# Three paired steps in each gated network instead of two, with the input's sums and two of four weight sums on GpSimd

## The chip, the core and the metric

The kernel runs on one core of a Trainium2 chip. The metric is the device time of one execution in microseconds (us), the median of several runs; lower is better. The engines are TensorE (PE in the profile, PEld for its weight loads), VectorE (DVE), ScalarE (ACT), GpSimd (POOL) and SyncE (SP, which issues the loads here). Each has its own instruction stream, worked off in order; they meet only at semaphores. PSUM is the memory that TensorE writes to (`bank` in the names); the rest of the tiles lie in SBUF.

## The reference

The program computes a block with four mixers and a mixture of experts, and then two layers of a second block. Each layer of the second block runs a gated network, a mixer and a second gated network. Those four gated networks, called ffn0 to ffn3, are what the change touches:

```python
def swiglu(x, w_gate, w_up, w_down):
    return (jax.nn.silu(x @ w_gate) * (x @ w_up)) @ w_down
# second block, both layers: 256 tokens, D_MODEL = 1024, D_FF = 2816, float32
f = swiglu(rms_norm_2(x, g[0]), ffn_w_gate[layer, 0], ffn_w_up[layer, 0], ffn_w_down[layer, 0])
x = x + 0.5 * rms_norm_2(f, g[1])
... # mixer_ab in layer 0, mixer_c in layer 1
f = swiglu(rms_norm_2(x, g[4]), ffn_w_gate[layer, 1], ffn_w_up[layer, 1], ffn_w_down[layer, 1])
x = x + 0.5 * rms_norm_2(f, g[5])
```

## The kernel before

**Split products.** Weights and activations are float32. Each operand is split into a high part (a rounded copy, made by ScalarE, `split` at L994) and a low part (the rest, a subtraction on VectorE, L1718), and a product is the sum of three matmuls: high by high, high by low, low by high. A low part costs VectorE one `tensor_tensor` of 128x2048 with both inputs in SBUF.

**Units.** All weights come as units of 1 MB (128 x 2048 float32). SyncE loads them in their order into a ring of 5 slots (`ring`), each once its slot is released: by default when the low part of the unit that lay there has been made (`RELEASE`, `load`). A network has 11 steps (`FFN_STEPS`) of 256 hidden columns. Step s uses two gate-and-up units (`place_A`: 3s-1 and 3s) and one down unit (`place_D`: 3s+4).

**A plain step** (`gate_up`, `turn`, `down_tile`). Per token tile t (0 or 1) TensorE does 24 matmuls of 128x512 for gate and up; ScalarE takes the silu, VectorE multiplies (`hid_made`, L2336); TensorE transposes the hidden values (`turn`, L3440), ScalarE and VectorE split them (`hid_in`, `hid_left`); 24 matmuls multiply by the down unit of the step before. Together 72 matmuls.

**A paired step** (`pair`, at the steps in `PAIRS`, 3 and 7 before) takes two steps, s and s+1, as a 2x2 block product: 2 token tiles by 2 column blocks, over 2 halves of the inner dimension. It uses seven block products where two plain steps use eight (Strassen's scheme in Winograd's form). A block product (`product`, L3483 to L3485) is 12 matmuls. For this it needs sums of the input blocks (`x_whole`, `x_sums`, `x_left`, once per network) and, per pair, four sums of the weight blocks b11, b21, b12, b22, which are the units a, a+1, a+3, a+4: t1 = b12 - b11 into the tile `w_sum` (which is `F`); t3 = b22 - b12 in b12's slot; t2 = t3 + b11 in b11's slot; t4 = b21 - t2 in b21's slot. t1 and t3 are made by `weight_sums` (L2371, L2373), t2 and t4 by `more_weight_sums` (L2378, L2380), all on VectorE in the step ahead of the pair. ScalarE makes the high parts of the sums in the single tile `sum_hi` in the order t2, t4, t1; VectorE the low parts (`ring_left`, `sum_left`, L2385).

The order of a pair on TensorE is: product with b11 (bank 4); `turn`; m6 (with t2; waits for its low part); product with b21; m7 (with t3; waits for `u2`, the sum that empties bank 7 into c_12); down, tile 0; m4 (with t4; waits for `u3`, the sum into c_22); down, tile 1; product with b22 (bank 4); `turn`; m5 (with t1; waits for its low part); down of step s. Semaphores `ffn_dve`, `ffn_act` and `ffn_pe` count each engine's steps by the lists `FFN_DVE`, `FFN_ACT`, `FFN_PE`. In the order of the program, "the step ahead" is the plain step right before a pair; with pairs at 3 and 7, two plain steps (5 and 6) lie between them.

GpSimd does only small things in this stretch: the root of the norms on 128x1 tiles (`post_power`, L876 to L882).

Of the kernel before, what the change touches and what calls it, by code (L numbers as in the profile page):

```python
# [5 lines left out]
FP32 = mybir.dt.float32  # L6
# [46 lines left out]
PAIRS = (3, 7)  # L53
# [217 lines left out]
def build(nc, x, gains, stream, small_1, cmp_w1, small_2, consts, slots, out):  # L271
# [3 lines left out]
    with ExitStack() as ctx:  # L275
# [524 lines left out]
        def _(sp):  # L800
# [66 lines left out]
        def _(pool):  # L867
# [89 lines left out]
        def _(act):  # L957
# [353 lines left out]
            def sparse():  # L1311
# [34 lines left out]
                for s in range(SPARSE_STEPS):  # L1346
# [4 lines left out]
                    act.activation(sil_m[:, :], bank[4][:, 0:UC], ACT.Silu, scale=rc[:, 6 * i + 4:6 * i + 5]).then_inc(S("m_silu"), 1)  # L1351
# [20 lines left out]
            def gated(name):  # L1372
# [20 lines left out]
                def x_sums_high():  # L1393
                    act.wait_ge(S("ffn_dve"), ffn_at(FFN_DVE, name, "s4"))
# [8 lines left out]
                def pair(i, s):  # L1403
# [10 lines left out]
                    split_at(3 * s + 4)  # L1414
                    act.wait_ge(S("ffn_pe"), ffn_at(FFN_PE, name, f"m4_{i}"))
# [22 lines left out]
                for s in range(1, last):  # L1438
# [7 lines left out]
                    silu(s, 1)  # L1446
                    if s + 1 in PAIRS:
# [3 lines left out]
                    if s + 2 == PAIRS[0]:  # L1451
                        x_sums_high()
# [252 lines left out]
        def _(dve):  # L1705
# [493 lines left out]
            def sparse():  # L2199
# [125 lines left out]
            def gated(name):  # L2325
# [23 lines left out]
                def x_whole():  # L2349
                    dve.wait_ge(S("h_lo"), HI0[name] + 4)  # L2350
# [1693 lines left out]
```

## Time and profile before

| | |
|---|---|
| median of 3 runs | 1794.06 us (1793.16 to 1794.82) |
| the profiled execution | 1793.34 us, span 1790.4 us |
| TensorE busy | 98% of the span |
| VectorE busy | 78% |
| ScalarE busy | 56% |
| GpSimd busy | 3% |
| the networks in the span | about 717 to 886, 1088 to 1256, 1273 to 1441, 1611 to 1780 us |

The time beside the span is 2.94 us. Busy time says that an engine had an instruction in hand. A matmul's duration (0.39 us) overlaps that of the next; what a matmul costs is the distance between two starts. The four networks run alike, to the same waits, so the working below follows one of them, ffn1, on its own clock.

### The profile page before, as it was taken

What the parts mean: (1) busy time and instruction counts of PE and PEld (TensorE: products, weight loads), DVE (VectorE), ACT (ScalarE), POOL (GpSimd) and SP (SyncE); (2) the same over time, 40 slices, a digit from 0 to 9 for tenths busy, and PEclk for the clock granted to TensorE, in tenths of its full rate; (3) what the DMA queues carried; (4) which work ended last, traced back from release to release, by engine and by line L of the source; (5) the groups of instructions that cost most, each with busy time, mean ns of one, the idle gap of its engine ahead of it and who ended that gap; (6) DMA issues with size and microseconds to landing.
All of it is one profiled execution on the core that took longest, in us unless ns stands there. A gap on an engine that the chain in (4) does not pass through costs nothing.

```text
span 1790.4 us, 25225 instructions
## 1 busy us (share of the span) xinstructions
PE 1754.3 (98%) x10314; PEld 1482.6 (83%) x10314; DVE 1389.7 (78%) x1646; ACT 995.0 (56%) x1206; POOL 58.1 (3%) x98
## 2 busy tenths in 40 slices
PE   9999999999999999999999999999999999999998
PEld 8998898888888887787898988778877878787877
DVE  5349877788898898978498779886897667879784
ACT  5446653577777676645452355555555456656453
POOL 0040000000000001000000000000100010010000
PEclk9999999999999999999999999999999999999999
DMA  9343344699899897373442016527443745234631
GB/s 383 118 165 136 119 148 149 240 359 351 337 351 354 334 372 293 123 280 139 190 152 108 27 53 230 225 83 312 180 170 136 305 143 187 72 141 150 273 147 76
DMA packets 51379, 363.01 MB, mean 203 GB/s; under 512 B 5697, under 2 KB 5825, under 8 KB 8642
## 3 DMA queue, kind: packets, MB, share of 16 engines
q1 hardware_dynamic: 50976, 359.24, 52.6%
q8 instruction: 82, 1.34, 0.3%
q10 hardware_dynamic: 290, 2.17, 0.3%
q14 instruction: 31, 0.25, 0.0%
HBM read 360.34 MB, written 1.05 MB: 202 GB/s over the span
## 4 chain that ended last, share of the span: by engine, by line
PE 79%; DVE 15%; ACT 3%; issue 1%; DMA 1%; POOL 0%; DVEq 0%; POOLq 0%; ACTq 0%
PE bank L2866 8%; PE bank L3424 4%; PE bank L3426 4%; PE bank L3425 4%; PE bank L3451 3%; PE bank L3449 3%; PE bank L3450 3%; PE bank L3278 3%; PE bank L3280 3%; PE bank L3279 3%; DVE w_a L1718 3%; PE bank L3483 3%; PE bank L2924 3%; PE bank L3484 2%; PE bank L3485 2%; PE bank L3295 2%
## 5 line engine op out<-in xcount | busy, mean ns | idle before, releaser
L1718 DVE TENSOR_TENSOR w_a<-ring,w_a 128x2048 fp32r<-128x2048 f32 x220 | 500.4, 2287 | 132.5 <-ACT w_a L994 131.8
L994 ACT ACTIVATE w_a<-ring 128x2048 fp32r<-128x2048 f32 x219 | 416.2, 1913 | 121.4 <-PE bank L3451 42.1
L1718 DVE TENSOR_TENSOR w_b<-ring,w_b 128x2048 fp32r<-128x2048 f32 x63 | 144.1, 2287 | 29.3 <-ACT w_b L994 29.2
L994 ACT ACTIVATE w_b<-ring 128x2048 fp32r<-128x2048 f32 x63 | 120.5, 1912 | 36.2 <-PE bank L3426 17.8
L2866 PE MATMUL bank<-h,w_a 128*128 128x256 f32 x1040 | 137.3, 285 | 1.0 <-DVE ring_lo L1823 1.0
L2866 PEld LDWEIGHTS bank<-h,w_a 128*128 128x128 f32 x1040 | 128.8, 191 | 4.1 <-issue 3.0
L3449 PE MATMUL bank<-w_a,hid 128*128 128x512 f32 x280 | 109.9, 393 | 0.0
L3451 PE MATMUL bank<-w_a,hid 128*128 128x512 f32 x280 | 109.2, 390 | 0.0
L3450 PE MATMUL bank<-w_a,hid 128*128 128x512 f32 x280 | 109.0, 389 | 0.0
L3424 PE MATMUL bank<-w_a,h 128*128 128x512 f32 x240 | 95.0, 396 | 0.5 <-DVE w_a L1718 0.5
L3426 PE MATMUL bank<-w_a,h 128*128 128x512 f32 x240 | 93.7, 390 | 0.0
L3425 PE MATMUL bank<-w_a,h 128*128 128x512 f32 x240 | 93.4, 389 | 0.0
L1391 ACT ACTIVATE sil<-bank,tiny 128x256 f32<-128x256 f32 x64 | 30.4, 474 | 101.0 <-PE bank L3426 98.9
L3278 PE MATMUL bank<-w_a,xg 128*128 128x512 f32 x192 | 77.1, 402 | 0.0
L3280 PE MATMUL bank<-w_a,xg 128*128 128x512 f32 x192 | 75.0, 391 | 0.0
L3279 PE MATMUL bank<-w_a,xg 128*128 128x512 f32 x192 | 74.8, 390 | 0.0
L978 ACT ACTIVATE arena<-bank 128x512 f32<-128x512 f32 (+2 forms) x47 | 26.8, 571 | 74.8 <-PE bank L2866 54.8
L881 POOL TENSOR_SCALAR tiny<-tiny 128x1 f32<-128x1 f32 x20 | 10.7, 533 | 1588.7 <-ACT junk L1012 1002.4
L3451 PEld LDWEIGHTS bank<-w_a,hid 128*128 128x128 f32 x280 | 52.6, 188 | 11.2
L2336 DVE SCALAR_TENSOR_TENSOR hid<-bank,tiny,sil 128x256 f32<-128x256 f32 x64 | 30.7, 480 | 39.9 <-ACT sil L1391 39.9
L3450 PEld LDWEIGHTS bank<-w_a,hid 128*128 128x128 f32 x280 | 52.6, 188 | 10.9
L3449 PEld LDWEIGHTS bank<-w_a,hid 128*128 128x128 f32 x280 | 52.6, 188 | 10.8
(648 smaller groups left out, 4201.1 us busy)
## 6 DMA issues: line engine op xcount, KB each, us to landing
ring<-in_stream SPq DMA_DIRECT2D x330, 1024.0 KB, 5.3
G<-in_gains SPq DMA_DIRECT2D x14, 512.0 KB, 7.8
cmp_area<-in_cmp_w ACTq DMA_DIRECT2D x1, 2048.0 KB, 11.3
sm<-in_small SPq DMA_DIRECT2D x1, 1582.0 KB, 12.0
con<-in_consts SPq DMA_DIRECT2D x1, 1032.0 KB, 15.9
X<-in_x SPq DMA_DIRECT2D x2, 512.0 KB, 4.0
out_x<-X SPq DMA_DIRECT2D x4, 256.0 KB, 2.0
sm<-in_small SPq DMA_DIRECT2D x1, 730.5 KB, 22.5
```

The costliest lines, as they stand in the source:

```text
L994: act.activation(w_slot(unit)[:, 0, :], ring[:, unit % RING, :], ACT.Copy).then_inc(S("w_hi"), 1)
L1718: dve.tensor_tensor(w_slot(unit)[:, 1, :], ring[:, unit % RING, :], w_slot(unit)[:, 0, :].bitcast(FP32), ALU.subtract).then_inc(S("w_lo"), 1)
L2866: ins = pe.matmul(ps, w(wp, k), xp[:, k, :], start=(a == 0 and k == 0), stop=(a == 2 and k == terms - 1))
L3278: pe.matmul(bank[4][:, :], x_hi, w[0][:, k, :], start=(half == 0 and k == 0), stop=False)
L3279: pe.matmul(bank[4][:, :], x_hi, w[1][:, k, :], start=False, stop=False)
L3280: ins = pe.matmul(bank[4][:, :], x_lo, w[0][:, k, :], start=False, stop=(half == 1 and k == 3))
L3424: pe.matmul(bank[4 + t][:, :], x_hi, w[0][:, k, :], start=first, stop=False)
L3425: pe.matmul(bank[4 + t][:, :], x_hi, w[1][:, k, :], start=False, stop=False)
L3426: ins = pe.matmul(bank[4 + t][:, :], x_lo, w[0][:, k, :], start=False, stop=end)
L3449: pe.matmul(ps, x_hi, w[0][:, f, d], start=(s == 0 and f == 0), stop=False)
L3450: pe.matmul(ps, x_hi, w[1][:, f, d], start=False, stop=False)
L3451: return pe.matmul(ps, x_lo, w[0][:, f, d], start=False, stop=(s == last and f == 1))
```

## The change

The pairs move from the steps 3 and 7 to the steps 2, 5 and 8, so only one plain step lies between two pairs, one (step 1) ahead of the first, and step 10 is the last. The five instructions that form the input's sums, and t3 and t1 of each pair, move from VectorE to GpSimd (`pair_sums`, called after `post_power` of the network). t1 is now formed as b22 - t2, which is the same sum; it waits for m6, and the slots of b11 and b22 are released to SyncE only once it is done. t2's low part goes to `w_sum_lo` (the tile `y_2`) instead of the ring. ScalarE makes the input sums' high part behind the second silu of step 1, and VectorE the low part there, ahead of t2, where both stood at the end of that step before. The semaphore `ffn_pool` counts GpSimd's steps; in the experts it stands in for `m_silu`.

```diff
-PAIRS = (3, 7)
+PAIRS = (2, 5, 8)
...
-                RELEASE[b11] = ("ffn_pe", ffn_at(FFN_PE, name, f"m6_{i}"))
+                SUMMED[b22] = ffn_at(FFN_POOL, name, f"t1_{i}")
+                RELEASE[b11] = ("ffn_pool", ffn_at(FFN_POOL, name, f"t1_{i}"))
                 RELEASE[b21] = ("ffn_pe", ffn_at(FFN_PE, name, f"m4_{i}"))
...
+            def pair_sums(name):
+                pool.wait_ge(S("h_lo"), HI0[name] + 4)
+                pool.tensor_tensor(x_raw, h_hi[:, :, :].bitcast(FP32), h_lo[:, :, :].bitcast(FP32), ALU.add).then_inc(S("ffn_pool"), 1)
+                own(name, "x_raw")
...
+                pool.tensor_tensor(x_sum[:, 0], a21, a22, ALU.add).then_inc(S("ffn_pool"), 1)
...
+                for i, s in enumerate(PAIRS):
+                    b11, _, b12, b22 = pair_units(name, s)
+                    for b in (b12, b22):
+                        pool.wait_ge(S(f"unit{b % RING}"), 16 * (b // RING + 1))
+                    pool.tensor_tensor(ring[:, b12 % RING, :], ring[:, b22 % RING, :], ring[:, b12 % RING, :], ALU.subtract)\
+                        .then_inc(S("ffn_pool"), 1)
+                    pool.wait_ge(S("ffn_dve"), ffn_at(FFN_DVE, name, f"t2_{i}"))
+                    pool.wait_ge(S("ffn_pe"), ffn_at(FFN_PE, name, f"m6_{i}"))
+                    pool.tensor_tensor(w_sum, ring[:, b22 % RING, :], ring[:, b11 % RING, :], ALU.subtract).then_inc(S("ffn_pool"), 1)
...
@@ scalar, gated
                     silu(s, 1)
+                    if s + 1 == PAIRS[0]:
+                        x_sums_high()
                     if s + 1 in PAIRS:
                         pair_ahead(PAIRS.index(s + 1), s + 1)
...
@@ vector, gated
-                    if s + 2 == PAIRS[0]:
-                        x_whole()
-                    if ahead is not None:
-                        weight_sums(ahead, s + 1)
                     split_at(3 * s + 3)
                     hid_made(s, 1)
+                    if s + 1 == PAIRS[0]:
+                        x_left()
                     if ahead is not None:
                         more_weight_sums(ahead, s + 1)
-                        ring_left(f"t2_hi_{ahead}", pair_units(name, s + 1)[0])
+                        sum_left(f"t2_hi_{ahead}", w_sum_lo, ring[:, pair_units(name, s + 1)[0] % RING, :])
...
@@ tensor, pair
-                    product(7, both[1], (sum_hi[:, :], ring_lo[:, b11 % RING, :]), True).then_inc(S("ffn_pe"), 1)
+                    product(7, both[1], (sum_hi[:, :], w_sum_lo), True).then_inc(S("ffn_pe"), 1)
```

GpSimd's instructions in ffn1, after the root of the norm (`tiny`), in the program after; before, nothing stands between that root and the next network's. `sm` holds the whole input, `H` its sums, `ring` the units, `F` is t1.

```order
L882 TENSOR_TENSOR tiny<-tiny 128x1 [waits s_pool_chain]
L952 TENSOR_TENSOR sm<-h 128x2048 [waits s_h_lo]
L955 TENSOR_TENSOR H<-sm 128x512 [waits s_ffn_pool]
L957 TENSOR_TENSOR H<-H,sm 128x512 [waits s_ffn_pool]
L958 TENSOR_TENSOR H<-sm 128x512
L960 TENSOR_TENSOR H<-sm,H 128x512 [waits s_ffn_pool]
L965 TENSOR_TENSOR ring<-ring 128x2048 [waits s_unit0,s_unit4]
L969 TENSOR_TENSOR F<-ring 128x2048 [waits s_ffn_pe,s_ffn_dve]
L965 TENSOR_TENSOR ring<-ring 128x2048 [waits s_unit4,s_unit3]
```

Seven instructions of 128x2048 and four of 128x512 per network are new on this engine, and t1 of a pair stands ahead of t3 of the next.

VectorE in ffn1 of the program before, from the second product of hidden values of step 0 (`hid<-bank5`) to the first input sums at the end of step 1; L1718 is a split.

```order
L2336 SCALAR_TENSOR_TENSOR hid<-bank5,tiny,sil 128x256 [waits s_silu]
L1718 TENSOR_TENSOR w_a<-ring,w_a 128x2048 [waits s_w_hi]
L2336 SCALAR_TENSOR_TENSOR hid<-bank4,tiny,sil 128x256 [waits s_silu]
L2343 TENSOR_TENSOR hid_2<-bank6,hid_2 128x2x256 [waits s_hid_hi]
L2351 TENSOR_TENSOR sm1<-h_2 128x2048 [waits s_h_lo]
L1718 TENSOR_TENSOR w_a<-ring,w_a 128x2048 [waits s_w_hi]
L2336 SCALAR_TENSOR_TENSOR hid<-bank5,tiny,sil 128x256 [waits s_silu]
L1718 TENSOR_TENSOR w_b<-ring,w_b 128x2048 [waits s_w_hi]
L2357 TENSOR_TENSOR H<-sm1 128x512 [waits s_ffn_dve]
```

The same place after (L1752 is now the split, L2370 and L2377 the hidden values): behind the second hidden values of step 1 stand the low part of the input sums (L2401), t2 and t4 (L2387, L2389), and t2's low part (L2394), because the first pair now follows this step.

```order
L2370 SCALAR_TENSOR_TENSOR hid<-bank5,tiny,sil 128x256 [waits s_silu]
L1752 TENSOR_TENSOR w_a<-ring,w_a 128x2048 [waits s_w_hi]
L2370 SCALAR_TENSOR_TENSOR hid<-bank4,tiny,sil 128x256 [waits s_silu]
L2377 TENSOR_TENSOR hid_2<-bank6,hid_2 128x2x256 [waits s_hid_hi]
L1752 TENSOR_TENSOR w_a<-ring,w_a 128x2048 [waits s_w_hi]
L2370 SCALAR_TENSOR_TENSOR hid<-bank5,tiny,sil 128x256 [waits s_silu]
L2401 TENSOR_TENSOR f_hi<-H,xs_hi 128x2048 [waits s_ffn_act]
L2387 TENSOR_TENSOR ring<-ring 128x2048 [waits s_unit1,s_ffn_pool]
L2389 TENSOR_TENSOR ring<-ring 128x2048 [waits s_ffn_dve]
L2394 TENSOR_TENSOR y_2<-ring,sum_hi 128x2048 [waits s_ffn_act]
L1752 TENSOR_TENSOR w_b<-ring,w_b 128x2048 [waits s_w_hi]
```

What moved: the sum of the whole input has left, the input sums' low part now waits for GpSimd through ScalarE right before the pair, and t2 waits for GpSimd's t3.

## Rows read from the trace of the kernel before

**Rows 1.** The page: busy us (share) xinstructions; the granted TensorE clock by slices.
```profile
PE 1754.3 (98%) x10314; PEld 1482.6 (83%) x10314; DVE 1389.7 (78%) x1646; ACT 995.0 (56%) x1206; POOL 58.1 (3%) x98
PEclk9999999999999999999999999999999999999999
```
**Rows 2.** Windows, ffn1: stretch, us, then busy us (x) per engine, clock, DMA.
```profile
1078.00:1256.00 178.00, 175.59 (x794) 144.03 (x793) 140.98 (x108) 94.94 (x84) 2.94 (x4) 1.00 0.55 213
```
**Rows 3.** Waits of TensorE: total us, times, longest us.
```profile
PE bank L3483 <- DVE ring_lo L2385: 9.6, 8, 1.4
```
**Rows 4.** Timeline of TensorE, ffn1: start us, duration us, instruction, idle before.
```profile
1088.03 0.39 PE L3424 MATMUL bank<-w_a,h 128*128 128x512 f32 x1
...
1093.25 0.39 PE L3426 MATMUL bank<-w_b,h 128*128 128x512 f32 x1
...
1104.82 0.39 PE L3424 MATMUL bank<-w_a,h 128*128 128x512 f32 x1
...
1124.35 0.60 PE L3440 MATMUL bank<-con,hid 128*128 128x128 f32 x4
1126.30 0.50 PE L3483 MATMUL bank<-sum_hi,xs_hi 128*128 128x512 f32 x1 [1.36 <-DVE ring_lo L2385]
```
**Rows 5.** Timeline of VectorE, first pair of ffn1.
```profile
1119.44 2.28 DVE L2378 TENSOR_TENSOR ring<-ring 128x2048 f32<-128x2048 f32 x1
1121.75 2.29 DVE L2380 TENSOR_TENSOR ring<-ring 128x2048 f32<-128x2048 f32 x1
...
1128.37 2.28 DVE L1718 TENSOR_TENSOR w_b<-ring,w_b 128x2048 fp32r<-128x2048 f32 x1
1130.57 0.68 DVE L2343 TENSOR_TENSOR hid<-bank,hid 128x512 fp32r<-128x512 f32 x1
...
1131.77 2.28 DVE L1718 TENSOR_TENSOR w_a<-ring,w_a 128x2048 fp32r<-128x2048 f32 x1
1133.97 0.48 DVE L2336 SCALAR_TENSOR_TENSOR hid<-bank,tiny,sil 128x256 f32<-128x256 f32 x1
1134.36 2.28 DVE L2385 TENSOR_TENSOR ring_lo<-ring,sum_hi 128x2048 fp32r<-128x2048 f32 x1
1136.56 0.68 DVE L2395 TENSOR_TENSOR sm<-bank,sm 128x512 f32<-128x512 f32 x1
```
**Rows 6.** Timeline of ScalarE, same pair.
```profile
1134.27 1.92 ACT L994 ACTIVATE w_a<-ring 128x2048 fp32r<-128x2048 f32 x1 [1.67 <-DMA ring<-in_stream]
1140.52 1.92 ACT L1416 ACTIVATE sum_hi<-F 128x2048 fp32r<-128x2048 f32 x1 [4.33 <-PE bank L3485]
```
**Rows 7.** Timeline of GpSimd, around 110 us, where it works beside VectorE.
```profile
107.07 2.00 POOL L925 TENSOR_TENSOR arena<-arena 128x1084 f32<-128x1084 f32 x1
109.14 1.54 POOL L930 TENSOR_TENSOR arena<-arena 128x810 f32<-128x810 f32 x1
...
119.19 0.94 POOL L930 TENSOR_TENSOR arena<-arena 128x264 f32<-128x264 f32 x1
120.21 1.08 POOL L933 TENSOR_TENSOR arena<-arena,con 128x16 f32<-128x16 f32 x1
...
123.43 0.73 POOL L937 TENSOR_TENSOR arena<-arena 128x256 f32<-128x256 f32 x1
```
**Rows 8.** Timeline of VectorE, the same stretch.
```profile
109.68 1.28 DVE L1840 TENSOR_SCALAR arena<-arena,tiny 128x512 f32<-128x512 f32 x1
...
119.44 1.78 DVE L1823 TENSOR_TENSOR ring_lo<-ring,w_a 128x1024 fp32r<-128x1024 f32 x1
...
121.14 1.23 DVE L1823 TENSOR_TENSOR ring_lo<-ring,w_a 128x1024 fp32r<-128x1024 f32 x1
```
**Rows 9.** Timeline of VectorE and GpSimd, start of ffn1.
```profile
1084.01 2.28 DVE L1718 TENSOR_TENSOR w_a<-ring,w_a 128x2048 fp32r<-128x2048 f32 x1
1084.49 1.87 POOL L876 TENSOR_SCALAR tiny<-tiny 128x1 f32<-128x1 f32 x1 [6.07 <-ACT junk L1147]
1086.44 0.56 POOL L877 TENSOR_TENSOR tiny<-tiny 128x1 f32<-128x1 f32 x1
1088.03 2.29 DVE L1718 TENSOR_TENSOR w_b<-ring,w_b 128x2048 fp32r<-128x2048 f32 x1 [1.32 <-ACT w_b L994]
```

More of the change, by code:

```diff
@@ L738, in sums_ready @@
             return "unit_used", D_UNITS[of] + (3 * STEPS[of] if of in STEPS else SQUARE)
+        SUMMED = {}
         for name in FFNS:
             for i, s in enumerate(PAIRS):
-                b11, b21, _, _ = pair_units(name, s)
-                RELEASE[b11] = ("ffn_pe", ffn_at(FFN_PE, name, f"m6_{i}"))
+                b11, b21, _, b22 = pair_units(name, s)
+                SUMMED[b22] = ffn_at(FFN_POOL, name, f"t1_{i}")
+                RELEASE[b11] = ("ffn_pool", ffn_at(FFN_POOL, name, f"t1_{i}"))
                 RELEASE[b21] = ("ffn_pe", ffn_at(FFN_PE, name, f"m4_{i}"))
@@ L939, in _, with own @@
                 src, dst = dst, src
+            def own(name, step):
+                pool.wait_ge(S("ffn_pool"), ffn_at(FFN_POOL, name, step))
+            def pair_sums(name):
+                pool.wait_ge(S("h_lo"), HI0[name] + 4)
+                pool.tensor_tensor(x_raw, h_hi[:, :, :].bitcast(FP32), h_lo[:, :, :].bitcast(FP32), ALU.add).then_inc(S("ffn_pool"), 1)
+                own(name, "x_raw")
+                a11, a12, a21, a22 = (x_raw[:, 4 * j:4 * j + 4, t * P:(t + 1) * P] for t in range(TT) for j in range(2))
+                pool.tensor_tensor(x_sum[:, 0], a21, a22, ALU.add).then_inc(S("ffn_pool"), 1)
+                own(name, "s1")
+                pool.tensor_tensor(x_sum[:, 1], x_sum[:, 0], a11, ALU.subtract).then_inc(S("ffn_pool"), 1)
+                pool.tensor_tensor(x_sum[:, 2], a11, a21, ALU.subtract).then_inc(S("ffn_pool"), 1)
+                own(name, "s2")
+                pool.tensor_tensor(x_sum[:, 3], a12, x_sum[:, 1], ALU.subtract).then_inc(S("ffn_pool"), 1)
+                for i, s in enumerate(PAIRS):
[7 more added lines that the diff above has]
+                    pool.tensor_tensor(w_sum, ring[:, b22 % RING, :], ring[:, b11 % RING, :], ALU.subtract).then_inc(S("ffn_pool"), 1)
             post_power("moe")
-            for name in ("ffn0", "ab"):
-                post_power(name)
+            post_power("ffn0")
+            pair_sums("ffn0")
+            post_power("ab")
             pool.wait_ge(S("x_turned"), 4 * NB["ab"] + 4)
@@ L948, in _ @@
             pool.memset(glu[:, :, 0:CONV_B - 1], 0.0).then_inc(S("zeroed_2"), 1)
-            for name in ("ffn1", "ffn2", "c"):
+            for name in ("ffn1", "ffn2"):
                 post_power(name)
-            for name in ("ffn3", "end"):
-                post_power(name)
+                pair_sums(name)
+            post_power("c")
+            post_power("ffn3")
+            pair_sums("ffn3")
+            post_power("end")
         @block.scalar
```

46 lines of the change are left out of this document (11 added, 35 removed).

## The prediction

> **What bounds the kernel now.** I read the busy shares first, then the granted clock, then TensorE's waits, then the timelines of one network. TensorE is busy for 98% of the span, and no slice shows a lowered clock [rows 1]. In ffn1 it is busy for 175.6 of 178.0 us, VectorE for 141.0 [rows 2]. So the networks run at TensorE's pace: 24 matmuls start from 1088.03 to 1093.25, 5.22 us over 23 distances, so a matmul costs 0.227 us [rows 4]. The only wait of note inside a pair is m6 for t2's low part: 9.6 us in eight pairs, 2.4 us per network [rows 3]. The reader should see that VectorE is not far behind, and that within a pair its chain is tight: a sum ends at 1123.96+2.28, and m6 starts at 1126.30 [rows 4, 5].
>
> All sums below are made against the profiled execution, 1793.34 us (0.7 us under the median of the runs). I count as no change what lies within 0.2%, or 3.6 us.
>
> **What the change saves.** A third pair per network replaces eight block products by seven: 12 matmuls of 0.227 us, 2.7 us per network. The old waits at m6 (2.4 us per network) are removed from the sum here and counted again below as they will then be. VectorE loses the sum of the whole input, four of 128x512 and two of 128x2048 per pair (2.28 us each, as those in [rows 5]), but that is worth only what TensorE waits for.
>
> **What GpSimd's instructions cost.** On GpSimd 128x1084 took 2.00 us and 128x256 took 0.73 us with little beside them [rows 7]. A line through both gives 1.53 ns per element, 3.5 us for 2048; in proportion to the 2.07 us between the starts of the first two it would be 3.9. I take 3.6 us for 128x2048 and 1.1 us for 128x512 (0.73 + 256 x 1.53 ns).
>
> **Do the two engines run side by side?** This decides the case. Four places say no, where VectorE reads two SBUF operands. At 119.44 a split of 128x1024 took 1.78 us, its twin at 121.14 took 1.23: it was held for 0.55 us, while GpSimd's instruction from 119.19 ran to 120.13 [rows 7, 8]. The `tensor_scalar` at 109.68 took 1.28 us and ended at 110.96, just after GpSimd's of 109.14 had ended at 110.68 [rows 7, 8]. The other way round, a 128x16 of GpSimd at 120.21 took 1.08 us, till that split had ended [rows 7, 8], and a 128x1 at 1084.49 took 1.87 us, till VectorE's split of 1084.01 ended at 1086.29 [rows 9]. So whoever started first keeps the other out for the whole instruction, and they take turns. VectorE instructions with an operand in PSUM (`hid_made`, `hid_left`, the sums into c) I take as not held.
>
> The Trainium skill says the same (SBUF — State Buffer, "SBUF: two separate sides"): the port pair is an exclusive lock, for a VectorE instruction with two SBUF inputs too, when the GpSimd one reads SBUF. That speaks against this change, since a sum moved away from VectorE blocks it for longer than it took there. It also gives 4497 ns for a GpSimd `tensor_tensor` of 2048 elements (GPSIMD Engine Reference, 3.1 Elementwise); no row here has that size. By it every hold below is 0.9 us longer, about 6 us more per network, and the sum would be some 25 us higher.
>
> **The start of a network**, ffn1's clock. GpSimd is free at 1087.0 [rows 9] and takes the whole input, 1087.1 to 1090.7. The split of unit 3, at 1088.03 before [rows 9], is held: 1090.7 to 1092.95. TensorE wants it after 12 matmuls from 1088.03, at 1090.75: a wait of 2.2 us. Then they take turns: input sum 1 to 1094.1, split to 1096.3, hidden values of tile 1 to 1096.8. TensorE's `turn`, due at 1093.5 + 2.2 = 1095.7, waits 1.1 us more. Together 3.3 us.
>
> **The first m6.** The turns go on: sum 2 to 1097.5, split 5 to 1099.7, sum 3 to 1100.9, sum 4 to 1102.1, split 6 to 1104.35, t3 on GpSimd to 1107.95. Now VectorE's low part of the input sums (to 1110.2), t2 (1112.4), t4 (1114.6) and t2's low part, to 1116.85, each 2.2 us from start to start. TensorE starts the pair at 1104.82 [rows 4] + 3.3 = 1108.1, does a product (2.7) and the transposes (0.35) and is ready for m6 at 1111.2. It waits 5.7 us. Without any hold the chain would still be late: high part of the input sums after the silu at 1100.1 to 1102.0, then 2.2 x 4 = 8.8 to 1110.8, against 1107.9: 2.9 us. From above, 0.9 us more per GpSimd instruction of 2048 gives 8.
>
> **The second and third m6.** VectorE no longer makes t1 and t3 ahead of the split of b21, so t2 could start 1.2 us sooner than at 1119.44. But only one plain step now lies ahead, and b22's load waits for a slot that is released late in the last pair; it lands in the middle of the step, so t3 (3.6 us) holds the split of b21 by about 1.0 us. I get a wait of 1.2 us each, as now; bounds 0.2 (no hold) and 3. 2.4 us per network.
>
> **m4 in each pair.** Count from the start of m6. VectorE makes two splits (to 4.4), GpSimd's t1 has been ready since 2.9 (m6 done) and runs 4.4 to 8.0; `hid_left` and u2 pass beside it (to 5.6); the split of b22 is held from 5.6 to 8.0 and ends at 10.2; hidden values (10.6), t4's low part (12.8), u3 (13.5). Before, the same chain ran without the hold, from 1131.77 to 1137.24 [rows 5]. TensorE is at m4 after m6, b21, m7 and down, four times 2.72, at 10.9. It waits 2.6 us, three times: 7.8 us per network. Lower bound 0 (no hold), upper 3.5 each. The unit in b11's slot is loaded only when t1 is done, 5 us later than before in the pair. ScalarE waited for it already, 1.67 us to 1134.27, but had then to wait for m4 until 1140.52 [rows 6], 4.3 us of cover, and m4 itself is late: I count nothing. If this cover goes, m5 is up to 3 us late.
>
> **The end.** The gain rows share memory with `sum_hi`, so SyncE's loads of gains and of the last two units wait for the last m5, now a pair later, in step 9 instead of 8. ScalarE and VectorE then split them behind; by my count they are just in time for the last down products. I take 0; up to 2 us per network if not.
>
> **Sum.** Per network 3.3 + 5.7 + 2.4 + 7.8 = 19.2 us of waits, less 2.4 of old waits, less 2.7 of matmuls: +14.1 us. Times four, +56: 1793.3 + 56.4 = 1849.7 us. I say 1850.
>
> **Rivals.**
> - *The engines run side by side after all*, at least for these instructions, the point from which it decides being any hold under about 0.5 us. Then per network the first m6 waits 2.9, the others 0.2, m4 0: 3.3 - 2.4 - 2.7 = -1.8, four times -7: 1786 us. For it: no row has two instructions of 2048 elements against each other. Against: [rows 7 to 9]. This is the faster side, 7%.
> - *The holds are there but VectorE's slack takes most of them.* It is idle for 37 of 178 us in ffn1 [rows 2], and a wait of TensorE at one place gives it time for the next. If m4's wait is 1 us and the start and first m6 cost 5 together: 5 + 2.4 + 3 - 5.1 = 5.3, times four: 1815 us. Against: VectorE's chain inside a pair has no gap of note before m4. 14%.
> - *The clock falls.* A wait of 5.7 us is four times the longest now at m6 [rows 3], and no slice shows a lowered clock now [rows 1]. If TensorE fell from 2.4 to 1.2 GHz behind each first m6 and lost, say, one block product's time (2.7 us) in going at half speed, 4 x 2.7 = 11 us: 1861. With longer holds beside it, up to 1880. 16%. The Trainium skill (TensorE: Matmul & The Clock Gate, Part 1) says that idleness lowers the clock; no row here shows it.
> - *The change doesn't show*: gains and holds cancel within 3.6 us. 3%.
>
> **How the numbers follow.** The forecast of holds as summed has 60%, with its own range 1838 to 1875 (a hold 0.4 us shorter or 0.9 longer in each of seven places per network, four times). For 8 in 10 I take in most of the clock's case and the upper part of the slack's: 1812 to 1880. Slower: 0.60 + 0.14 + 0.16 = 0.90, same 0.03, faster 0.07.
>
> **What would show it.** GpSimd's sums with starts and ends against VectorE's splits: splits of 128x2048 lasting up to 5.9 us instead of 2.28, GpSimd's 128x2048 at 3.5 us or more. TensorE's waits: m6 about 5.7 us in the first pair and 1 to 2 in the others; a new one at m4 of about 2.6 us, twelve times; one of 2 us in step 1. If splits stay at 2.28 us beside GpSimd, the forecast's main step is wrong. If TensorE's waits total under 10 us more than before, the sizes are.

## The result, and the profile after

The changed kernel takes 1892.45 us (median of 4 runs, 1890.68 to 1898.52), the kernel before 1793.61 us beside it (4 runs). The ratio is 1.056, 95% interval 1.054 to 1.058: about 99 us slower. The forecast was 1850 us with 1812 to 1880. The direction was right, and the time lies 12 us above the range. The profiled execution took 1893.17 us, its span is 1891.4 us.

The page, against [rows 1]:

```profile
PE 1779.3 (94%) x10266; PEld 1494.1 (79%) x10266; DVE 1497.8 (79%) x1654; ACT 1019.3 (54%) x1222; POOL 232.1 (12%) x142
PEclk9999999999999998999999999999899999999999
```

48 matmuls fewer, and yet TensorE is busy 25.0 us longer; it is idle 112.1 us (1891.4 - 1779.3) instead of 36.1. So of 101.0 us more span, 76.0 are new waits. The other 25.0 are slower work, with the 10.8 us (four times 2.7) that 48 matmuls fewer save already taken off. By the prediction it would have been 67.2 us of waits (4 x 19.2 less 9.6) and 10.8 less of work. VectorE is busy 108.1 us longer, although the input's sums, t3 and t1 were taken from it: in this view the duration of an instruction includes the time for which it is held.

TensorE's waits (total us, times, longest), against [rows 3]; L3486 is the product of both m6 (`y`, the low part of t2) and m4 (`sm`, u3), L3427 the gate products, L3443 the `turn`:

```profile
PE bank L3486 <- DVE y L2394: 49.5, 12, 6.3
PE bank L3486 <- DVE sm L2404: 22.4, 12, 2.0
PE bank L3427 <- DVE w_a L1752: 6.8, 2, 3.9
...
PE bank L3427 <- DVE w_b L1752: 2.9, 1, 2.9
PE bank L3443 <- DVE hid L2370: 2.3, 1, 2.3
```

All the waits that the prediction named are there, in its places; only at the start there is one wait per network, of 2.3 to 3.9 us, where it had two (2.2 and 1.1). Now the groups of instructions (busy us, mean ns of one | idle before):

```profile
L1752 DVE TENSOR_TENSOR w_a<-ring,w_a 128x2048 fp32r<-128x2048 f32 x220 | 574.5, 2624 | 143.9 <-ACT w_a L1027 143.2
...
L969 POOL TENSOR_TENSOR F<-ring 128x2048 f32<-128x2048 f32 x12 | 56.7, 4723 | 181.4 <-PE bank L3488 181.4
L965 POOL TENSOR_TENSOR ring<-ring 128x2048 f32<-128x2048 f32 x12 | 55.4, 4618 | 255.2 <-DMA ring<-in_stream 255.2
...
L955 POOL TENSOR_TENSOR H<-sm 128x512 f32<-128x512 f32 x4 | 12.8, 3209 | 0.3
```

The mean split rose from 2287 to 2624 ns. GpSimd needs 4.6 to 4.7 us for 128x2048, where the prediction took 3.6. The first two of its 128x512 last 3.2 us each, but the last one takes 1.30 us, with no split beside it (the row at 1126.31 below): the rest is waiting for a split. Both engines in ffn1, first VectorE, then GpSimd (start us, duration us, instruction, idle before), against [rows 5] and [rows 9]:

```profile
1112.90 5.72 DVE L1752 TENSOR_TENSOR w_b<-ring,w_b 128x2048 fp32r<-128x2048 f32 x1 [1.32 <-ACT w_b L1027]
1118.54 3.36 DVE L1752 TENSOR_TENSOR w_a<-ring,w_a 128x2048 fp32r<-128x2048 f32 x1
...
1128.51 5.82 DVE L1752 TENSOR_TENSOR w_a<-ring,w_a 128x2048 fp32r<-128x2048 f32 x1 [2.33 <-ACT w_a L1027]
...
1149.92 6.31 DVE L1752 TENSOR_TENSOR w_a<-ring,w_a 128x2048 fp32r<-128x2048 f32 x1
...
1187.45 5.62 DVE L1752 TENSOR_TENSOR w_b<-ring,w_b 128x2048 fp32r<-128x2048 f32 x1 [3.43 <-ACT w_b L1027]
```

```profile
1111.85 4.62 POOL L952 TENSOR_TENSOR sm<-h 128x2048 f32<-128x2048 f32 x1
1116.55 3.21 POOL L955 TENSOR_TENSOR H<-sm 128x512 f32<-128x512 f32 x1
...
1126.31 1.30 POOL L960 TENSOR_TENSOR H<-sm,H 128x512 f32<-128x512 f32 x1
1127.56 4.62 POOL L965 TENSOR_TENSOR ring<-ring 128x2048 f32<-128x2048 f32 x1
...
1149.35 4.73 POOL L969 TENSOR_TENSOR F<-ring 128x2048 f32<-128x2048 f32 x1 [17.16 <-PE bank L3488]
...
1186.31 4.61 POOL L965 TENSOR_TENSOR ring<-ring 128x2048 f32<-128x2048 f32 x1 [32.23 <-DMA ring<-in_stream]
```

Read them in pairs. GpSimd's sum of 1127.56 ends at 1132.18; the split of 1128.51 lasts till 1134.33, 2.15 us more, which is about its own 2.28. The distance of the two ends is 2.15 us for 1111.85 with 1112.90, for 1149.35 with 1149.92 and for 1186.31 with 1187.45, too. A VectorE instruction with an operand in PSUM isn't held: one of 128x512 (u2) started at 1205.11, inside GpSimd's sum from 1205.00 to 1209.72, and took its usual 0.68 us. None of those that run inside a GpSimd sum in this trace takes over 0.7 us.

The waits at the end of that, on TensorE, against [rows 4], and four stretches (length, then busy us and count of PE, PEld, DVE, ACT, POOL, then the granted clock, DMA share, GB/s), against [rows 2]:

```profile
1143.71 0.80 PE L3486 MATMUL bank<-sum_hi,xs_hi 128*128 128x512 f32 x1 [5.92 <-DVE y L2394]
...
1200.25 0.50 PE L3486 MATMUL bank<-sum_hi,xs_hi 128*128 128x512 f32 x1 [3.52 <-DVE y L2394]
```

```profile
1119.00:1122.00 3.00, 3.00 (x8) 2.32 (x8) 3.00 (x2) 0.00 (x0) 2.92 (x2) 0.50 0.73 251
1144.00:1148.00 4.00, 4.00 (x10) 3.13 (x10) 4.00 (x3) 3.44 (x4) 0.00 (x0) 0.50 0.00 0
1148.00:1152.00 4.00, 4.00 (x15) 3.16 (x15) 3.35 (x4) 1.92 (x1) 2.65 (x1) 0.81 0.00 0
1152.00:1156.00 4.00, 4.00 (x19) 3.23 (x18) 4.00 (x1) 0.47 (x1) 2.08 (x1) 1.00 0.26 37
```

Behind the wait of 2.9 us in step 1 and behind the 5.9 us at m6, TensorE runs at 0.50 of its clock, 1.2 GHz: 10 matmuls start in 4 us where 19 do at full clock. The page's digit per slice (47 us) hides that. In the 4 us behind each of the twelve waits at m6, those of 2.5 us too, the mean clock is 0.50 to 0.69; behind those at m4, of 1.6 to 2.0 us, it stays at 1.00. Added up from 700 us on, (1 - clock) x busy time is 34 us; before, it is 3.4 us over the whole span.

### The profile page after: what moved, and what is told of

It is laid out like the page before. It is cut to its first block, busy times and chain, and to the rows that moved or that the text cites. A ratio compares the mean times of both kernels' runs of the same rounds, so it can differ in the third digit from the quotient of the medians.

```text
span 1891.4 us, 25277 instructions
## 1 busy us (share of the span) xinstructions
PE 1779.3 (94%) x10266; PEld 1494.1 (79%) x10266; DVE 1497.8 (79%) x1654; ACT 1019.3 (54%) x1222; POOL 232.1 (12%) x142
## 3 DMA queue, kind: packets, MB, share of 16 engines
HBM read 360.34 MB, written 1.05 MB: 191 GB/s over the span
## 4 chain that ended last, share of the span: by engine, by line
PE 66%; DVE 23%; ACT 4%; issue 4%; DMA 2%; POOL 1%; DVEq 0%; POOLq 0%; ACTq 0%
PE bank L2869 7%; DVE w_a L1752 7%; PE bank L3281 3%; PE bank L3283 3%; PE bank L3282 3%; DVE w_b L1752 3%; PE bank L2927 2%; PE bank L3486 2%; PE bank L3427 2%; PE bank L3454 2%; PE bank L3429 2%; PE bank L3428 2%; PE bank L3452 2%; PE bank L3453 2%; PE bank L3487 2%
## 5 line engine op out<-in xcount | busy, mean ns | idle before, releaser
L1752 DVE TENSOR_TENSOR w_a<-ring,w_a 128x2048 fp32r<-128x2048 f32 x220 | 574.5, 2624 | 143.9 <-ACT w_a L1027 143.2
L1752 DVE TENSOR_TENSOR w_b<-ring,w_b 128x2048 fp32r<-128x2048 f32 x63 | 174.4, 2768 | 32.6 <-ACT w_b L1027 32.4
L886 POOL TENSOR_SCALAR tiny<-tiny 128x1 f32<-128x1 f32 x20 | 10.7, 535 | 1078.4 <-ACT junk L1045 491.9
L3486 PE MATMUL bank<-sum_hi,xs_hi 128*128 128x512 f32 x96 | 49.8, 519 | 49.5 <-DVE y L2394 49.5
L965 POOL TENSOR_TENSOR ring<-ring 128x2048 f32<-128x2048 f32 x12 | 55.4, 4618 | 255.2 <-DMA ring<-in_stream 255.2
L3427 PE MATMUL bank<-w_a,h 128*128 128x512 f32 x192 | 77.4, 403 | 6.8 <-DVE w_a L1752 6.8
L969 POOL TENSOR_TENSOR F<-ring 128x2048 f32<-128x2048 f32 x12 | 56.7, 4723 | 181.4 <-PE bank L3488 181.4
L3429 PE MATMUL bank<-w_a,h 128*128 128x512 f32 x192 | 76.0, 396 | 0.0
L3428 PE MATMUL bank<-w_a,h 128*128 128x512 f32 x192 | 75.9, 395 | 0.0
L1434 ACT ACTIVATE sum_hi<-ring 128x2048 fp32r<-128x2048 f32 x12 | 23.0, 1914 | 85.4 <-DVE ring L2387 85.4
L3486 PEld LDWEIGHTS bank<-sum_hi,xs_hi 128*128 128x128 f32 x96 | 23.2, 242 | 57.1 <-DVE y L2394 52.3
## 6 DMA issues: line engine op xcount, KB each, us to landing
sm<-in_small SPq DMA_DIRECT2D x1, 730.5 KB, 22.4
```

Of the source, the lines that this page charges most:

```text
L1752: dve.tensor_tensor(w_slot(unit)[:, 1, :], ring[:, unit % RING, :], w_slot(unit)[:, 0, :].bitcast(FP32), ALU.subtract).then_inc(S("w_lo"), 1)
L3427: pe.matmul(bank[4 + t][:, :], x_hi, w[0][:, k, :], start=first, stop=False)
L3428: pe.matmul(bank[4 + t][:, :], x_hi, w[1][:, k, :], start=False, stop=False)
L3429: ins = pe.matmul(bank[4 + t][:, :], x_lo, w[0][:, k, :], start=False, stop=end)
```

## The experiments

The theory: a GpSimd instruction that reads SBUF and a VectorE instruction with two SBUF inputs take turns; this makes VectorE's chain late at three places (the start, m6, m4), and the clock adds to it. The rivals were that GpSimd's results merely come late, that three pairs are too dense in themselves, and that the clock, not VectorE, makes the pair long. The kernel before ran beside each, with medians of 1791.4 to 1794.1 us, and the ratios are to these.

**Is it the turns, and what do three pairs cost without them?**

`small_sums`: GpSimd's sums cover 16 columns.

```diff
-pool.tensor_tensor(w_sum, ring[:, b22 % RING, :], ring[:, b11 % RING, :], ALU.subtract)
+pool.tensor_tensor(w_sum[:, 0:16], ring[:, b22 % RING, 0:16], ring[:, b11 % RING, 0:16], ALU.subtract)
...
-act.activation(xs_hi[:, :, :, :], x_sum, ACT.Copy)
+act.activation(xs_hi[:, :, :, :], other(h_hi), ACT.Copy)
```

> The changed kernel with each of GpSimd's sums cut to its first 16 columns; every wait and every place stays, so the products run on values that are not the sums (the high and low parts of the input sums and of t1 are taken from other tiles of the same size). Theory H (a GpSimd sum shuts VectorE's two-input instructions out for its whole length, and the waits that this makes let TensorE's clock fall): the holds are gone, splits last 2.28 us, m4 waits about 0, the first m6 about 3 us, the others under 0.5, the clock falls little: 1780 to 1792 us. Theory S (the layout does it: one plain step between pairs, a slot released late, input sums' parts right ahead of the first pair, whatever engine makes the sums): waits of 4 us at m6 and 2 us at m4 stay, 1870 us or more.

1791.49 us (10 runs), ratio 0.9998 (0.9987 to 1.0009). Span 1787.6 us, and the waits:

```profile
PE bank L3490 <- DVE y L2398: 13.0, 12, 2.8
```

The first m6 of each network waits 2.83 us, as worked out for the chain without a hold (2.9), the others 0.19 to 0.29; m4 waits for nothing and starts 11.22 us after m6. So the third pair is worth next to nothing even with sums that cost nothing, and all of the loss comes from what GpSimd's sums do.

`writes_only`, `writes_longer` and `writes_same`: the sums are replaced by GpSimd writing a constant to the same tiles, with the same waits, for about 3.7, 5.6 and 4.8 us per 128x2048. A write reads nothing.

```diff
-pool.tensor_tensor(w_sum, ring[:, b22 % RING, :], ring[:, b11 % RING, :], ALU.subtract)
+for n in range(FILLS):   # 2; 3; 2 and one of 1100 columns
+    pool.memset(w_sum, 0.0)
```

> The changed kernel with each of GpSimd's sums replaced by two fills (memset) of the same tile, one after the other: GpSimd is busy for about 3.8 us for 128x2048 instead of 4.6, and reads nothing of SBUF; the sums are zero, so the products are. Theory H in the form that only a GpSimd instruction that reads SBUF shuts VectorE out: splits stay at 2.28 us beside it, m4 waits about 0, only t3 and the input sums come late: 1785 to 1800 us. Theory H in the form that any GpSimd instruction on SBUF shuts it out: splits of up to 5 us, m4 waits about 1.5 us, 1850 us or more. Theory S: 1870 or more, whatever the form.

1791.67 us (10 runs), ratio 1.0 (0.999 to 1.0011); splits at 2287 ns.

> As the run with two fills per sum, but with three, 5.4 us for 128x2048, longer than the 4.6 us of the real sum. If only reading shuts VectorE out: splits at 2.28 us, TensorE waits a little longer at the first m6 for t3; 1790 to 1805 us. If it was the shorter time of the two fills that made that run fast: 1830 us or more.

1830.3 us (1827.88 to 1836.71), ratio 1.0224 (1.0203 to 1.0244). That is above the expected range of 1790 to 1805 us: splits still take 2288 ns, but the waits are back.

```profile
PE bank L3492 <- DVE y L2400: 27.0, 12, 3.9
PE bank L3449 <- DVE hid L2376: 16.5, 12, 1.5
```

The lateness of GpSimd's results alone can thus cost, if it is long enough. The next run has writes as long as the sums really were.

> Leaves out of the computation: every sum of GpSimd is replaced by writes of a constant to the same tile, with the same waits and order. They are sized to last about as long as the sums really did, some 4.6 to 4.7 us for 128x2048 (two whole ones of 1.82 us and one of 1100 columns) and 1.3 us for 128x512. They read nothing, so VectorE isn't held; what is left is that GpSimd's results and the slots that they release come late. If the hold is what costs, the splits stay at 2.29 us, m4 waits for nothing, m6 waits 2.8 to 3.2 us in the first pair and under 1 in the others, and the time is 1791 to 1808 us. Rival (the lateness of GpSimd's own results costs, and the hold is beside the point): 1830 us or more, as with writes of 5.6 us (1830).

1803.09 us (1801.42 to 1803.27, 4 runs), ratio 1.005 (1.0033 to 1.0066). Two whole writes and one of 1100 columns last 4.76 us from start to end; their groups, and TensorE's waits:

```profile
L957 POOL MEMSET F<- 128x2048 f32 x24 | 43.6, 1815 | 134.1 <-PE bank L3495 133.4
...
L957 POOL MEMSET F<- 128x1100 f32 x12 | 12.2, 1019 | 0.7
```

```profile
PE bank L3493 <- DVE y L2401: 14.0, 12, 2.8
PE bank L3450 <- DVE hid L2377: 7.1, 12, 0.8
```

Splits are at 2288 ns, and m4 waits for nothing. So lateness by itself is worth 11.6 us (1803.09 - 1791.49), and the other 89 us of the changed kernel's loss come only when GpSimd reads. The 11.6 us also lie elsewhere: m4 to m5 takes 9.6 us more in all than in `small_sums`, where the changed kernel loses 1.3. What is late there is the unit in b11's slot, loaded only once the writes in t1's place are done (at 1172.63 us in ffn1's second pair). ScalarE waits for it, and the hidden values come late behind it. ScalarE's row:

```profile
1177.59 1.92 ACT L1034 ACTIVATE w_b<-ring 128x2048 fp32r<-128x2048 f32 x1 [6.59 <-DMA ring<-in_stream]
```

In `small_sums` that wait is 2.80 us. In the changed kernel m4 is itself late by then, and covers it.

`copies`: every sum is a copy of one of its inputs, one SBUF operand instead of two.

```diff
-pool.tensor_tensor(w_sum, ring[:, b22 % RING, :], ring[:, b11 % RING, :], ALU.subtract)
+pool.tensor_copy(w_sum, ring[:, b22 % RING, :])
```

> Leaves out of the computation: every sum of GpSimd is a copy of one of its two inputs, with the same waits, order and output tile. It reads one SBUF operand instead of two. If one read is enough to keep VectorE out, splits of 128x2048 still last up to 4 us or more (2.28 us plus what is left of a copy), and the time lies between those of the kernel with the sums cut and the one with them whole, by how long a copy takes: at about 2 us each 1805 to 1850 us. If only two-operand reads hold VectorE, splits stay at 2.29 us, m4 doesn't wait, and the time is 1788 to 1800 us.

1805.56 us (2 runs), ratio 1.007 (1.005 to 1.009). The copy of t1's place and the split of b22 in ffn1, VectorE and then GpSimd:

```profile
1123.01 3.33 DVE L1752 TENSOR_TENSOR w_a<-ring,w_a 128x2048 fp32r<-128x2048 f32 x1
```

```profile
1122.29 1.90 POOL L969 COPY F<-ring 128x2048 f32<-128x2048 f32 x1 [16.27 <-PE bank L3488]
```

The copy ends at 1124.19, the split at 1126.34, 2.15 us later: one operand read holds it too, only for a shorter time, since a copy takes 1.90 us.

**Which instruction costs what?**

`input_sums_cut`: the five sums of the input cover 16 columns, t3 and t1 are whole.

```diff
-pool.tensor_tensor(x_raw, h_hi[:, :, :].bitcast(FP32), h_lo[:, :, :].bitcast(FP32), ALU.add)
+pool.tensor_tensor(x_raw[:, 0, 0:16], h_hi[:, 0, 0:16].bitcast(FP32), h_lo[:, 0, 0:16].bitcast(FP32), ALU.add)
```

> The changed kernel with the whole input and its four sums cut to 16 columns on GpSimd, t3 and t1 of every pair as they are (the products run on an input that is not the sums). By my terms the start (3.3 us) and half of the first m6's wait (3 us) go, and the clock's fall in step 1 with them (2 us): 8 us per network, 1855 to 1868 us. Rival (the first m6 is late because t3 holds the split ahead of it, not because of the input sums): only the start goes, 1870 to 1880.

1875.46 us (1871.66 to 1876.84), ratio 1.0462 (1.0446 to 1.0478): 17 us less than the changed kernel, about half of the 32 us (8 per network) expected, and in the rival's range. The first m6 still waits 5.7 to 6.4 us. In ffn1, GpSimd's t3 and the split of b21:

```profile
1119.47 4.63 POOL L969 TENSOR_TENSOR ring<-ring 128x2048 f32<-128x2048 f32 x1 [9.81 <-DMA ring<-in_stream]
```

```profile
1120.39 5.86 DVE L1756 TENSOR_TENSOR w_a<-ring,w_a 128x2048 fp32r<-128x2048 f32 x1 [2.77 <-ACT w_a L1031]
```

GpSimd had been idle for 9.81 us; here t3 starts when b22 has landed, and then holds the split ahead of t2. In the changed kernel the first t3 of each network has no idle time before it: in ffn1 it follows the last input sum (1126.31 + 1.30), 0.9 us after b22 landed. In both kernels t3 starts 6.9 us ahead of the pair's first product (at 1126.34 and 1134.46), so cutting the input's sums doesn't help the first m6.

`t3_cut`: only t3 is cut.

```diff
-pool.tensor_tensor(ring[:, b12 % RING, :], ring[:, b22 % RING, :], ring[:, b12 % RING, :], ALU.subtract)
+pool.tensor_tensor(ring[:, b12 % RING, 0:16], ring[:, b22 % RING, 0:16], ring[:, b12 % RING, 0:16], ALU.subtract)
```

> Leaves out of the computation: b22 - b12 (t3) is summed for 16 of its 2048 columns. All other sums of GpSimd are whole. Theory (t3, held back until b22 has landed, makes m6 late in all three pairs by holding the split of b21): the waits at m6 fall from about 6 to 2.8 to 3.8 us in the first pair and from about 3 to under 0.8 in the other two, 16 to 22 us in all twelve; the clock stays up behind most of them, but m6 to m4 stays at 14 to 15 us since t1's hold is there, so the wait at m4 rises to 30 us or more in twelve. Time 1850 to 1865 us. Rival (the input's sums make the first m6 late): the first m6 still waits 5 us or more, and the time is over 1868.

1858.43 us (1854.51 to 1864.1, 4 runs), ratio 1.0375 (1.0357 to 1.0393):

```profile
PE bank L3486 <- DVE sm L2404: 32.7, 12, 3.0
PE bank L3486 <- DVE y L2394: 13.0, 12, 2.8
```

The waits at m6 are those of `small_sums`, 2.83 us in the first pairs and 0.2 to 0.3 in the others. So t3 alone makes m6 late, in the first pair too, where the prediction blamed the input's sums as well. m4 then waits 2.7 us each, 14.3 us behind m6 in ten pairs of twelve, and in six pairs m4 to m5 takes 10.2 to 10.4 us instead of 8.8, at a lowered clock.

`t1_cut`: only t1 is cut; its readers take the high part of the input sums.

```diff
-pool.tensor_tensor(w_sum, ring[:, b22 % RING, :], ring[:, b11 % RING, :], ALU.subtract)
+pool.tensor_tensor(w_sum[:, 0:16], ring[:, b22 % RING, 0:16], ring[:, b11 % RING, 0:16], ALU.subtract)
```

> Leaves out of the computation: b22 - b11 (t1) is summed for 16 of its 2048 columns, and its two readers take the high part of the input sums instead, which has the same shape. All other sums of GpSimd are whole. Theory (GpSimd and VectorE take turns at reading SBUF, and t1 is what holds the split of b22 before m4): the wait at m4 (22.4 us in twelve pairs) goes to under 2 us, m6 starts 11.2 us before m4 at full clock and 12 to 13.5 behind a long m6 wait, and the waits at m6 stay at 45 to 52 us; twelve times 2.5 to 3.9 us less than 1892: 1845 to 1862 us. Rival (the low clock behind m6 makes the pair long, not VectorE's chain): m6 to m4 stays at 14 us or more with the wait at m4 gone, and the time is over 1870.

1861.76 us (1855.07 to 1862.89, 4 runs), ratio 1.0385 (1.0368 to 1.0403). No wait at m4 is left, and those at m6 stay:

```profile
PE bank L3486 <- DVE y L2394: 48.3, 12, 6.4
```

Here the clock can be seen by itself, since VectorE is in time. The stretch from m6 to m4 in the first pair of ffn1, in this kernel, and in `small_sums`:

```profile
1136.55:1148.99 12.44, 12.44 (x49) 10.12 (x49) 11.90 (x9) 8.05 (x7) 0.22 (x1) 0.89 0.24 84
```

```profile
1111.28:1122.50 11.22, 11.22 (x48) 9.03 (x49) 10.95 (x8) 7.95 (x7) 1.24 (x1) 1.00 0.26 93
```

The same work takes 1.2 us longer at a mean clock of 0.89; over the twelve pairs the stretches come to 148.1 us against 136.1.

**Is the clock a cost of its own?** `filled_waits`: 24, 12 and 12 matmuls whose result nobody reads stand ahead of the three m6.

```diff
+pe.wait_ge(S("ffn_act"), ffn_at(FFN_ACT, name, "s_hi"))
+for _ in range((24, 12, 12)[i]):
+    pe.matmul(bank[7][:, :], h_hi[:, 0, 0:P], xs_hi[:, 0, :, :], start=True, stop=True)
 sum_ready(f"t2_lo_{i}")
```

> The changed kernel with matmuls put ahead of m6 that do nothing for the result (24 in the first pair of a network, 12 in the others, 128x512 into the bank that m6 overwrites), so that TensorE works through most of its wait for t2's low part. All waits on data stay. Theory C (idling at m6 makes the granted clock fall from 2.4 to 1.2 GHz, and that costs more than a quarter of the slowdown): the clock falls only in step 1 of the networks, and about 25 us come back: 1862 to 1875 us. Rival (the low clock lies over stretches in which VectorE is the later one anyway, so it costs nothing): within 5 us of the changed kernel, 1887 to 1897.

1895.45 us (1892.53 to 1895.87, 4 runs), ratio 1.0574 (1.0558 to 1.059): nothing gained.

```profile
PE bank L3486 <- DVE sm L2404: 34.6, 12, 3.0
...
PE bank L3486 <- DVE y L2394: 5.5, 9, 1.1
```

From m6 to m4 the mean clock is now 0.97 or more in all twelve pairs. These stretches come to 170.9 us instead of 182.0, only 11 us less: VectorE takes up to 14.3 us for each, so m4 waits longer (34.6 us instead of 22.4). Behind those waits the clock now fell in nine pairs of twelve, and m4 to m5 comes to 121.6 us instead of 105.4, 16 us longer. One such stretch, where the changed kernel took 8.77 us at full clock:

```profile
1214.36:1224.69 10.33, 10.33 (x40) 8.29 (x41) 5.82 (x5) 4.97 (x4) 0.00 (x0) 0.83 0.47 182
```

The time came out in the rival's range, but not for its reason alone: the theory's condition, a clock that falls only in step 1, wasn't met, and slow work still comes to 24.5 us. The run shows that filling moved the slow stretches from behind m6 to behind m4. It doesn't show that they cost nothing; `t1_cut` above has them cost 12 us where VectorE is in time. What it and the 14.3 us bear out is smaller: where VectorE is late anyway, part of the 34 us of slow work covers time that would be a wait, so the 34 us can't be added to the waits in full.

**Which part of the change?** `pairs_on_vector`: three pairs, all sums on VectorE. `two_pairs_on_gpsimd`: the changed kernel with the pairs at 3 and 7; so beside the engine of the sums, the later place of the input sums' high and low parts and the later release of two slots stay in.

```diff
-PAIRS = (3, 7)      # the kernel before, x_whole, x_sums and x_left moved to the steps 0 and 1
+PAIRS = (2, 5, 8)
```

> The kernel before with pairs at the steps 2, 5 and 8, all sums on VectorE: the whole input and its sums behind the second hidden values of step 0, their high part on ScalarE and low part on VectorE right ahead of the first pair, as in the changed kernel. Theory H: no m4 waits, later m6 about 1.3 us, the first m6 about 7 us since VectorE has all the sums in step 1, some clock lost behind it: 1810 to 1840 us. Theory S: as slow as the changed kernel, 1870 or more.

1826.29 us (1825.07 to 1828.74), ratio 1.0193 (1.0175 to 1.0211):

```profile
PE bank L3481 <- DVE ring_lo L2385: 37.2, 12, 7.2
```

```diff
-PAIRS = (2, 5, 8)   # the changed kernel
+PAIRS = (3, 7)
```

> The changed kernel with pairs at the steps 3 and 7 again: only the engine of the sums is changed against the kernel before. Theory H: about 3 us of wait per network in step 1, m4 waits 1.9 us in each of 8 pairs, clock falls in step 1 (about 2 us each network): 1815 to 1835 us. Theory S: within 5 us of the kernel before.

1844.22 us (1842.74 to 1845.23), ratio 1.0292 (1.0275 to 1.0309), above the 1815 to 1835 expected:

```profile
PE bank L3486 <- DVE sm L2404: 18.9, 8, 3.0
PE bank L3486 <- DVE y L2394: 12.1, 8, 2.8
```

Against the kernel before, the stretches from m6 to m4 come to 116.0 us instead of 89.8: 3.3 us more per pair, where 1.9 were expected. Up to the first m6 of the networks 24 us are lost. The m6, though, cost little here: 2.83 us in the first pair of each network and 0.2 in the second, none of the 2.5 to 3.8 us of the changed kernel. The reason is where t3 falls. With two plain steps ahead it runs while VectorE has no split in hand (one ends at 1196.94, the next starts at 1203.31, and both take 2.29 us):

```profile
1196.71 4.71 POOL L965 TENSOR_TENSOR ring<-ring 128x2048 f32<-128x2048 f32 x1 [43.59 <-DMA ring<-in_stream]
```

So both parts lose by themselves: moving the sums 52 us with two pairs, the third pair 34 us with the sums on VectorE. There the sums of the input and of the weights are all made in step 1, and the first m6 waits 7.2 us.

**A version slightly ahead of both.** `early_t1`: the kernel before, with t1 of the second pair made by VectorE a step earlier, where it has idle time.

```diff
+                    if s + 2 == PAIRS[1]:
+                        first_sum(1, s + 2)      # t1 of the second pair
```

> The kernel before, with one instruction moved: VectorE makes t1 of the second pair (b12 - b11) at the end of the plain step two ahead of it, where it waits for ScalarE, instead of one ahead. It should start t2 up to 1.1 us sooner, and the second m6 wait fall from 1.04 us to about 0 in four networks: 3 to 4 us faster, a ratio of 0.998. Rival (b12 or its slot is not loaded that early, and the wait for it delays the hidden values): same or 2 us slower.

1788.83 us (1787.23 to 1792.68, 11 runs) against 1791.39 (15 runs), ratio 0.9986 (0.9977 to 0.9995): a gain of 0.14%, small, but its interval leaves 1 out.

```profile
PE bank L3491 <- DVE ring_lo L2391: 6.2, 8, 1.4
```

The second pair's wait at m6 falls from 1.05 to 0.20 us, 3.4 us in all; 2.6 come out.

## Why the prediction was right and wrong

`small_sums` has the program of the changed kernel without the cost of its sums, so the changed kernel can be compared with it stretch by stretch, from the starts of m6, m4 and m5 in the twelve pairs of both traces. In us of span, four networks; the prediction's column takes its waits less those that it gave without holds (2.9 and 0.2 at m6):

| term | predicted | measured |
|---|---|---|
| third pair, no holds | -7.2 | -2.8 |
| up to the first m6 (start, 3.3, and m6) | +24.4 | +32.6 |
| second and third m6 | +8.0 | +23.9 |
| m6 to m4 | +31.2 | +45.9 |
| m4 to m5 | 0 | +1.3 |
| sum | +56.4 | +100.9 |

- **The mechanism was right.** The engines take turns for whole instructions (`writes_same` against the changed kernel), and TensorE pays at the start, at m6 and at m4. Splits lasted up to 6.3 us. That VectorE's instructions with an operand in PSUM pass beside GpSimd was taken, and holds. One of the four places given for the turns is weak: the `tensor_scalar` at 109.68 reads one large operand, not two. The other three carry the point. The rivals "side by side", "slack absorbs" and "doesn't show" fell.
- **The start and the first m6.** 3.3 + 5.7 us per network, 36.0 in all; the waits shown are 12.0 at the start (6.8 + 2.9 + 2.3) and 24.0 at the first m6 (5.9, 5.9, 6.3, 5.9). The sizes came out nearly right, and that was partly luck. At the start there is one wait per network where two were worked out. In the first pair t3 was to run behind the last split, for 3.6 us; it runs ahead of it, for 4.6 us, and holds it. The attribution was wrong: "The turns go on" through the input's sums to t3, but `t3_cut` brings the first m6 to 2.83 us with all input sums in place, and cutting these leaves it near 6. The 8 us that the table has beyond these waits are put down to TensorE at 1.2 GHz in step 1 and after.
- **The later m6: this step failed.** "t3 (3.6 us) holds the split of b21 by about 1.0 us" puts the start of t3 2.6 us ahead of that split, from a landing of b22 in the middle of the step. In ffn1's second pair t3 starts 1.14 us ahead and runs 4.61, and the split lasts 5.62 us: a hold of 3.3 us. Over the eight later pairs the lead is 0.9 to 2.1 us, 1.5 in the mean, and the hold 2.3 to 3.6, 3.0 in the mean. So of the 2 us missing per pair about one is the lead and one GpSimd's duration. The eight waits are 2.5 to 3.8 us, 25.5 in all, and 1.7 in all without t3. It was the largest miss, 15.9 us. The upper bound given (3) lay just under the mean wait (3.2); the value taken lay nearer the lower one, without a row for the lead on which it hung. With two plain steps between the pairs the hold is gone altogether (`two_pairs_on_gpsimd`).
- **m4: mis-sized.** Forecast 2.6 us over a pair at full clock. Where the clock is full behind m6 (ten pairs of `t3_cut`; none of the changed kernel), the stretch is 14.3 us instead of 11.22: 3.1 us, twelve times 37.1, with GpSimd at 4.7 us instead of 3.6. The other 8.8 us are pairs of 14.5 to 15.8 us, in which TensorE is slow before it is late.
- **GpSimd's duration.** 3.6 us came from a line through two short rows, though the proportion from the longest one gave 3.9. 4.6 to 4.7 us were measured. The sums of 16, 512 and 2048 columns in these runs (0.22, 1.30 and 4.62 us) lie on one line, 0.2 us and 2.16 ns per column; the row of 1084 elements, 2.00 us, lies 0.5 us below it and bent the estimate. Why is open. The Trainium skill's 4497 ns (GPSIMD Engine Reference, 3.1 Elementwise) was quoted and priced at 25 us more; that would have given 1875, inside the range but still below the result. The means here, 4618 and 4723 ns, are 3% and 5% above it.
- **The clock.** It was a rival with 16% and an own price of 11 us, up to 1880 with longer holds. The clock did fall, behind waits of 2.5 us as well as of 5.9, and what the table has beyond the holds and the waits, 8 + 9 us, is put down to it. Forecast and rival were set against each other, as if only one could be, while the waits of the one bring about the other: with 19 us of waits per network forecast, the clock's part belonged in the sum. The Trainium skill's rule that idleness lowers the clock (TensorE: Matmul & The Clock Gate, Part 1) agrees with this trace (0.50 behind the wait of 5.92 us).
- **The end, and b11's slot.** Counted as nothing, and no wait of TensorE showed there; m4 to m5 is 8.8 us against 8.7. The late load is real, as `writes_same` shows, but m4's own wait covers it here.
- **The gain.** -7.2 us was forecast without holds, -2.8 came in span. The saving is small partly because each first m6 waits 2.83 us in any case, instead of 1.36 before. That isn't the early place of the pair, since `two_pairs_on_gpsimd`, with its first pair at step 3, shows the same 2.83 us: it is the low part of the input sums, which now stands right ahead of t2, t4 and t2's low part on VectorE; the later pairs, which lack it, wait 0.2 us.

Cut one at a time, t3 is worth 34 us, t1 31 and the input's sums 17: 82 of the 101 us. The other 19 us are not the price of one of them, since a cut lets another cost grow: with t3 cut, m4's wait grows from 22.4 to 32.7 us, and m4 to m5 from 105.4 to 114.6 us at a lowered clock. No run cuts two of the three, so these 19 us are not split further. Nor does a run separate the clock's 17 us from the waits that bring it about. `writes_longer` takes 27 us more than `writes_same` with 0.8 us more per write: the waits at m6 (27.0 against 14.0) and at L3449 (16.5 against 7.1) give 22 us of it, and slow work (10.7 against 6.5 us) another 4.

## What to carry to other kernels

Moving a two-input VectorE sum to GpSimd doesn't take load off VectorE when both read SBUF: a VectorE split that comes up meanwhile is held until GpSimd's instruction ends, here 4.6 us for a sum that took VectorE 2.3. It costs VectorE nothing only where no such split comes up for that long, as with t3 in `two_pairs_on_gpsimd`. What decides is when it starts: look for what releases it (here a landing unit) and place it on VectorE's clock before pricing the hold. And when a forecast adds waits of 2.5 us and more to TensorE, as at m6 here, put the lower clock that can follow them into the sum, but only for stretches in which TensorE is what is late.

## What the runs showed of the hardware that was not expected

- GpSimd instructions that only write SBUF don't hold VectorE: writes of 128x2048 (1.82 us) beside splits left these at 2.29 us. Those that read one operand do (split 3.33 us beside a copy), as those that read two.
- A GpSimd copy of 128x2048 float32 took 1.90 us, a sum of two operands 4.6 us: 2.7 us more, which is more than the whole copy.
- VectorE instructions with an operand in PSUM pass beside a GpSimd sum: 128x512 in 0.68 us, as before.
- TensorE's clock was at 1.2 GHz behind every wait of 2.5 us and more at m6 in the changed kernel, in a stream that was busy for the rest. Elsewhere waits as long left it up: in `small_sums` three of the four waits of 2.83 us at m6 left it up (11.22 us to m4), and one didn't (12.62 us).
